# Decoder step with a mixture of experts: last pass's rows added on TensorE, the others' rows added by Pool beside it

## What is computed

```python
def moe_swiglu(h, router, w_gate, w_up, w_down):
    logits = jnp.einsum('btd,de->bte', h, router).astype(jnp.float32)
    top_v, top_i = lax.top_k(logits, TOP_K)
    gate = jax.nn.softmax(top_v, axis=-1)
    combine = jnp.einsum('btk,btke->bte', gate, jax.nn.one_hot(top_i, N_EXPERTS, dtype=jnp.float32))
    out = jnp.zeros(h.shape, jnp.float32)
    for e in range(N_EXPERTS):
        he = jax.nn.silu(h @ w_gate[e]) * (h @ w_up[e])
        out = out + combine[..., e:e + 1] * (he @ w_down[e])
    return out.astype(h.dtype)
```

## Time and profile before

| | us |
|---|---|
| median of 3 runs | 1996.9 (1996.71 to 1997.59) |
| the profiled execution's own time | 1998.28 |
| its span, first to last instruction | 1995.7 |
| TensorE busy in the span | 1961.5 |
| VectorE, ScalarE, POOL busy | 474.0, 298.4, 143.3 |

### The profile page before, as it was taken

How to read it: one execution, slowest core, us unless ns; L and a number is a source line. 1 busy time by engine, 2 the same in 40 slices (tenths; PEclk the granted TensorE clock), 3 DMA queues, 4 the chain that set the end, 5 groups by cost and what they waited for, 6 DMA issues and landing times.

```text
span 1995.7 us, 40349 instructions
## 1 busy us (share of the span) xinstructions
PE 1961.5 (98%) x17109; PEld 1400.9 (70%) x17109; DVE 474.0 (24%) x1223; ACT 298.4 (15%) x741; POOL 143.3 (7%) x246
## 2 busy tenths in 40 slices
PE   8999999999999999999999999999999999999996
PEld 6877777777777777777777476777777675647453
DVE  1353564220000134338433210101001001001011
ACT  2263231100000125422211100000000000000000
POOL 2221011000000000210000300000000000000000
PEclk9999999999999999999999999999999999999998
DMA  9645556464433344554532899999999999999996
GB/s 323 225 164 205 205 175 239 152 233 161 141 133 128 129 146 167 188 193 144 198 130 103 317 415 420 410 419 411 419 413 417 416 413 421 409 421 409 414 420 239
DMA packets 100121, 553.26 MB, mean 277 GB/s; under 512 B 13872, under 2 KB 30288, under 8 KB 41328
## 3 DMA queue, kind: packets, MB, share of 16 engines
q1 hardware_dynamic: 84432, 491.96, 62.9%
q0 software_dynamic: 12720, 48.97, 6.8%
q10 hardware_dynamic: 2800, 9.83, 1.4%
HBM read 532.08 MB, written 24.89 MB: 279 GB/s over the span
## 4 chain that ended last, share of the span: by engine, by line
PE 88%; issue 8%; DVE 2%; DMA 1%; POOL 0%; ACT 0%; POOLq 0%; DVEq 0%; SPq 0%
PE bank L490 38%; PE bank L1052 36%; PE bank L657 3%; PE bank L601 2%; PE bank L688 1%; PE bank L713 1%; PE bank L701 1%; DMA pages<-in_slc_pages 1%; PE bank L541 1%; PE bank L783 1%; PE bank L810 0%; DVE tmp L1916 0%; PE bank L851 0%; PE bank L919 0%; DMA wring<-in_wstream 0%
## 5 line engine op out<-in xcount | busy, mean ns | idle before, releaser
L1052 PE MATMUL bank<-wring,phase_region 128*32 128x512 f32 (+3 forms) x10112 | 868.4, 506 | 0.0
L1052 PEld LDWEIGHTS bank<-wring,phase_region 128*32 128x32 f32 x10112 | 561.7, 110 | 306.5 <-issue 148.2
L490 PE MATMUL bank<-xn,wring 128*128 128x288 f32 x2256 | 567.0, 409 | 9.8 <-DMA wring<-in_wstream 9.2
L490 PEld LDWEIGHTS bank<-xn,wring 128*128 128x128 f32 x2256 | 425.6, 191 | 134.1 <-DMA wring<-in_wstream 9.2
L490 PE MATMUL bank<-phase_region,wring 128*128 128x288 f32 x608 | 148.0, 406 | 0.6 <-DVE phase_region L2096 0.6
L2214 DVE TENSOR_TENSOR tmp<-phase_region,bank 128x512 f32<-128x512 f32 (+1 forms) x48 | 28.6, 595 | 500.9 <-PE bank L1052 500.9
L490 PEld LDWEIGHTS bank<-phase_region,wring 128*128 128x128 f32 x608 | 115.4, 190 | 32.9 <-DVE phase_region L2096 1.1
L1293 ACT ACTIVATE phase_region<-bank 128x512 f32<-128x512 f32 (+14 forms) x124 | 52.8, 464 | 425.2 <-PE bank L1052 296.5
L1584 ACT ACTIVATE phase_region<-bank 128x512 f32<-128x512 f32 (+1 forms) x48 | 26.1, 544 | 531.2 <-PE bank L1052 531.2
L2227 DVE COPY phase_region<-bank 32x256 f32<-32x256 f32 x32 | 13.5, 421 | 263.0 <-PE bank L1052 262.7
L657 PE MATMUL bank<-pages,wring 128*64 128x128 f32 (+1 forms) x1024 | 58.9, 276 | 0.0
(11 more groups left out here) (353 smaller groups left out, 1192.1 us busy)
## 6 DMA issues: line engine op xcount, KB each, us to landing
wring<-in_wstream SPq DMA_DIRECT2D x448, 1024.0 KB, 8.1
y_rows<-phase_region ACTq DMA_DIRECT2D x25, 384.0 KB, 7.5
pages<-in_cmp_pages POOLq DMA_DIRECT2D x64, 128.0 KB, 4.4
pages<-in_cmp_pages SPq DMA_DIRECT2D x64, 128.0 KB, 3.0
pages<-in_slc_pages SPq DMA_DIRECT2D x64, 128.0 KB, 4.4
pages<-in_slc_pages POOLq DMA_DIRECT2D x64, 128.0 KB, 4.8
out_win_keep<-in_win_rows POOLq DMA_DIRECT2D x2, 4064.0 KB, 26.6
pages<-in_win_kT POOLq DMA_DIRECT2D x4, 1024.0 KB, 5.3
```

Source lines behind the costliest of these rows:

```text
L490: mm = nc.tensor.matmul(ps[:, 0:width], wb, rhs(k), start=(k == 0), stop=(k == n - 1))
L1052: mm = nc.tensor.matmul(ps[QT * q:QT * q + QT, out0:out0 + n], lhsT, wring[:, a:a + n], start=start, stop=stop)
```

## The change

The expert whose pass is the last one is treated apart. A token's late row may lie in that pass; for such a token the late row's number is bent to a row of zeros, and its place in the last pass is kept (`rel`). POOL brings these places into a row of 288 numbers on 96 partitions through DRAM (`last_of`, `of_last`), and VectorE compares them with the partition's number (times four, as the constant stands) to a one-hot matrix `one_hot`, 96 x 288. After the loop TensorE multiplies `one_hot` with `yS`, three tiles by two halves of 512 columns, into six banks; the first half waits only for ScalarE's first copy into `yS` (`half_ready`). VectorE adds each product, times `w_late`, to `res`, and SP sends each tile out in two halves.

Both gathers of POOL now wait for the same count of written passes, all but the last, and so follow each other during the last pass, the late one into `pages`. POOL itself multiplies and adds their rows to `res`, twelve operations, and VectorE waits for all of them (`res_sum`) after its loop. At the very end POOL waits for the last pass's rows to be written, which nobody reads any more.

```diff
@@ -302,7 +302,7 @@
         xrow = view(xn_, 0, 3, D // 4)
         xq = view(pages, 0, 3, D)
         res = [view(xn_, D, D), view(oS_, 0, D), view(oC_, 0, D)]
-        early, late = view(reg, 0, 3, D), view(reg, 3 * D, 3, D)
+        early, late = view(reg, 0, 3, D), view(pages, 0, 3, D)
         he = rm(3, NFE * QT)
         xe = rm(3, KD * QT)
         pick = rm(3, CAP)
@@ -320,6 +320,10 @@
         edge = rm(ROW_COLS)
         at_row, at_strip = rm(2 * 3), rm(2 * 3)
         strips = rm(2 * 3, ROW_COLS)
+        of_last = view(reg, rm.at - 2 * 3 * ROW_COLS, T)
+        one_hot = rT
+        base, rel, away = rm(1), rm(3), rm(3)
+        FIN_BANKS = (0, 1, 2, 3, 6, 7)
 
         def C(name, rows=P):
             a, n = CONST_AT[name]
@@ -1098,6 +1102,19 @@
                             mm.then_inc(doneB, 1)
                     assert met[0] == EXP_SLOTS - 1
 
+            pe.wait_ge(S["one_ready"], 1)
+            pe.wait_ge(S["half_ready"], n_it * UNROLL)
+            for hf in range(2):
+                if hf == 1:
+                    for part in range(2):
+                        b, n = loop_released(("dn", part), 0)
+                        per = loop_count(("dn", part), 1) - n
+                        pe.wait_ge(b, n_it * (UNROLL * per) + (n - per))
+                for tt, (t0, n) in enumerate(TILES):
+                    ps = psum[(moe_base[0] + FIN_BANKS[3 * hf + tt]) % 8]
+                    nc.tensor.matmul(ps[0:n, 0:512], one_hot[0:CAP, t0:t0 + n], yS[0:CAP, 512 * hf:512 * hf + 512], start=True, stop=True)\
+                        .then_inc(S["fin"], 1)
+
 
         @block.sync
         def _(sp):
@@ -1164,10 +1181,11 @@
                 pass_slots(i + 1, ex2, 0, RING)
             ex = sp.value_load(passes[0:1, bass.ds(n_pass - 1, 1)], min_val=0, max_val=NE - 1)
             pass_slots(n_pass - 1, ex, RING, EXP_SLOTS)
-            for tt, (t0, n) in enumerate(TILES):
-                sp.wait_ge(S["tile_ready"], tt + 1)
-                sp.dma_start(y_out[t0:t0 + n, :], res[tt][0:n, :]).then_inc(S["y_done"], 16)
-            sp.wait_ge(S["y_done"], 48)
+            for hf in range(2):
+                for tt, (t0, n) in enumerate(TILES):
+                    sp.wait_ge(S["tile_ready"], 3 * hf + tt + 1)
+                    sp.dma_start(y_out[t0:t0 + n, 512 * hf:512 * hf + 512], res[tt][0:n, 512 * hf:512 * hf + 512]).then_inc(S["y_done"], 16)
+            sp.wait_ge(S["y_done"], 6 * 16)
 
 
         @block.gpsimd
@@ -1260,6 +1278,11 @@
             pool.wait_ge(S["scattered"], 6 * 16)
             for q in range(4):
                 pool.dma_start(rows_of[QT * q:QT * q + QT, :], tok_of).then_inc(S["rows_of_in"], 16)
+            pool.wait_ge(S["last_ready"], 1)
+            for tt, (t0, n) in enumerate(TILES):
+                pool.dma_start(last_of[t0:t0 + n, :], rel[0:n, tt:tt + 1]).then_inc(S["last_out"], 16)
+            pool.wait_ge(S["last_out"], 48)
+            pool.dma_start(of_last[0:CAP, :], last_of.rearrange("t o -> o t").to_broadcast([CAP, T])).then_inc(S["last_in"], 16)
             n_it = pool.value_load(passes[0:1, 33:34], min_val=NE // UNROLL, max_val=MAX_PASSES // UNROLL)
             quarter_rows = tok_rows.rearrange("t (q c) -> (t q) c", q=4)
             with pool.Fori(0, n_it) as it:
@@ -1272,11 +1295,23 @@
                             .then_inc(S["xrow_in"], 16)
             for j, (dst, name) in enumerate(((early, "early_in"), (late, "late_in"))):
                 pool.wait_ge(S["turn_ready"], n_it * UNROLL + 1 + j)
-                pool.wait_ge(S["y_rows_out"], n_it * (16 * UNROLL) + 16 * (MAX_PASSES + j))
+                pool.wait_ge(S["y_rows_out"], n_it * (16 * UNROLL) + 16 * MAX_PASSES)
                 nc.gpsimd.tensor_tensor(turn[0:1, 1:2], turn[0:1, 0:1], turn[0:1, 0:1], ALU.add).then_inc(S["turn_ready"], 1)
                 for tt, (t0, n) in enumerate(TILES):
                     pool.indirect_dma_start(dst[0:n, tt, :], None, y_rows, bass.IndirectOffsetOnAxis(ap=row_of[0:n, 3 * j + tt:3 * j + tt + 1], axis=0))\
                         .then_inc(S[f"{name}{tt}"], 16)
+            sums = 0
+            for dst, name, weight in ((early, "early_in", w_early), (late, "late_in", w_late)):
+                for tt, (t0, n) in enumerate(TILES):
+                    pool.wait_ge(S[f"{name}{tt}"], 16)
+                    nc.gpsimd.tensor_tensor(dst[0:n, tt, :], dst[0:n, tt, :], weight[0:n, tt, :].to_broadcast([n, D]), ALU.mult).then_inc(S["res_sum"], 1)
+                    sums += 1
+                    pool.wait_ge(S["res_sum"], sums)
+                    nc.gpsimd.tensor_tensor(res[tt][0:n, :], res[tt][0:n, :], dst[0:n, tt, :], ALU.add).then_inc(S["res_sum"], 1)
+                    sums += 1
+                    pool.wait_ge(S["res_sum"], sums)
+            pool.wait_ge(S["y_rows_out"], n_it * (16 * UNROLL) + 16 * (MAX_PASSES + 1))
+            nc.gpsimd.tensor_tensor(turn[0:1, 1:2], turn[0:1, 0:1], turn[0:1, 0:1], ALU.add).then_inc(S["turn_ready"], 1)
 
 
         @block.scalar
@@ -1585,7 +1620,7 @@
                     act.wait_ge(S["y_rows_out"], i * 16 + BLANKS)
                     act.wait_ge(*loop_filled(("dn", 0), i))
                     ps = psum[loop_bank(("dn", 0))]
-                    copy(yS[0:CAP, 0:512], ps[0:CAP, 0:512])
+                    copy(yS[0:CAP, 0:512], ps[0:CAP, 0:512]).then_inc(S["half_ready"], 1)
                     copy(yS[0:QT, 512:D], ps[CAP:P, 0:512]).then_inc(bank_free[loop_bank(("dn", 0))], 1)
                     act.wait_ge(*loop_released(("dn", 0), i))
                     act.wait_ge(*loop_released(("dn", 1), i))
@@ -2190,7 +2225,6 @@
             link(V.tensor_tensor(w_early, rg2, w_early, ALU.add))
             for j, op in enumerate((ALU.min, ALU.max)):
                 link(V.tensor_tensor(at_row[:, 3 * j:3 * j + 3], rm1.rearrange("p a b -> p (a b)"), rm2.rearrange("p a b -> p (a b)"), op))
-            link(V.tensor_copy(row_of[:, :], at_row))
 
             link(V.tensor_scalar(edge, C("iota")[:, 1:ROW_COLS + 1], float(QT), None, ALU.mult))
             link(V.tensor_tensor(strips, bc(at_row, 2, ROW_COLS), bc(edge, 1, 6), ALU.is_ge))
@@ -2198,10 +2232,21 @@
             link(V.tensor_scalar(at_strip, at_strip, float(QT * ROW_COLS - 1), None, ALU.mult))
             link(V.scalar_tensor_tensor(at_strip, at_row, float(ROW_COLS), at_strip, ALU.mult, ALU.subtract))
             link(V.tensor_copy(scat[:, :], at_strip))
+            link(V.tensor_scalar(base, tabf[:, 32:33], float(CAP), float(-CAP), ALU.mult, ALU.add))
+            link(V.tensor_tensor(rel, at_row[:, 3:6], base.to_broadcast([P, 3]), ALU.subtract))
+            link(V.tensor_scalar(away, rel, 0.0, None, ALU.is_ge))
+            link(V.tensor_scalar(at_strip[:, 3:6], at_row[:, 3:6], -1.0, float(MAX_PASSES * CAP), ALU.mult, ALU.add))
+            link(V.tensor_tensor(away, away, at_strip[:, 3:6], ALU.mult))
+            link(V.tensor_tensor(at_row[:, 3:6], at_row[:, 3:6], away, ALU.add))
+            link(V.tensor_copy(row_of[:, :], at_row))
             signal("rows_ready")
+            link(V.tensor_scalar(rel, rel, 4.0, None, ALU.mult))
+            signal("last_ready")
             n_it = dve.value_load(passes[0:1, 33:34], min_val=NE // UNROLL, max_val=MAX_PASSES // UNROLL)
             dve.wait_ge(S["rows_of_in"], 4 * 16)
             V.tensor_tensor(slot_row[:, :], rows_of[:, 3:6], C("quarter").to_broadcast([P, 3]), ALU.add).then_inc(S["idx_ready"], 1)
+            dve.wait_ge(S["last_in"], 16)
+            V.tensor_scalar(one_hot[0:CAP, :], of_last[0:CAP, :], C("tok_row", CAP)[:, 0:1], None, ALU.is_equal).then_inc(S["one_ready"], 1)
 
             with dve.Fori(0, n_it) as it:
                 for i in [it * UNROLL + n for n in range(UNROLL)]:
@@ -2226,13 +2271,13 @@
                     for q, (t, n0) in enumerate(DN_B):
                         last = V.tensor_copy(yS[QT * t:QT * t + QT, n0:n0 + 256], psum[b][QT * q:QT * q + QT, 0:256])
                     last.then_inc(bank_free[b], 1)
-            for tt, (t0, n) in enumerate(TILES):
-                dve.wait_ge(S[f"early_in{tt}"], 16)
-                link(V.scalar_tensor_tensor(res[tt][0:n, :], early[0:n, tt, :], w_early[0:n, tt, :], res[tt][0:n, :], ALU.mult, ALU.add))
-            for tt, (t0, n) in enumerate(TILES):
-                dve.wait_ge(S[f"late_in{tt}"], 16)
-                V.scalar_tensor_tensor(res[tt][0:n, :], late[0:n, tt, :], w_late[0:n, tt, :], res[tt][0:n, :], ALU.mult, ALU.add)\
-                    .then_inc(S["tile_ready"], 1)
+            dve.wait_ge(S["res_sum"], 12)
+            for hf in range(2):
+                for tt, (t0, n) in enumerate(TILES):
+                    dve.wait_ge(S["fin"], 3 * hf + tt + 1)
+                    ps = psum[(moe_base[0] + FIN_BANKS[3 * hf + tt]) % 8]
+                    r = res[tt][0:n, 512 * hf:512 * hf + 512]
+                    V.scalar_tensor_tensor(r, ps[0:n, 0:512], w_late[0:n, tt, :], r, ALU.mult, ALU.add).then_inc(S["tile_ready"], 1)
 
 
 
```

5 lines of the change are left out of this document (3 added, 2 removed).

## The result

The changed kernel took **2002.06 us** (median of 13 runs, 2000.23 to 2004.12), the kernel before in the same comparison 1998.19 us (13 runs). The ratio is 1.0022, 95% interval 1.0016 to 1.0029: slower by 0.22%, where 1990.9 us and a gain were forecast.

What follows compares the result with a forecast made beforehand. TensorE, 98% busy, and DMA were taken as level in the expert loop, with a tail of waits behind it. 3.3 us lost to the late gather less 9.28 won gives -6.0: 1990.9 us, range 1987.6 to 1995.0.

Steps and rivals of the forecast that it cites:

- Tail, removed and added: After the loop: 13.42 us of row write, wait, gather and sums replaced by 4.14 us, 9.28 us won.
- The closing: From last sum to end of span: output transfer and close of the program, left unchanged at 4.36 us.
- Ahead of the loop: Before the expert loop: POOL's writes and read back take 12.5 us, VectorE ready about 1139; price 0, cover 8 us.
- rival 3: Ahead of the loop: long write and read-back chain makes VectorE late, TensorE lacks free banks, kernel slower; chance 3%.
- The late gather: Last pass: 288 rows, 1.18 MB, gathered behind the early set, delay the weights; 3.3 us lost.
- TensorE's way out of its loop: At loop end: TensorE falls through without a fetch wait; 0 taken, 0.9 us kept for the range.
- POOL's twelve sums: Last pass: two operations per tile and set, 12 us in all, nobody waiting before 1981; price 0.

Runs made afterwards that it cites:

- e1: Changed kernel, but POOL's last wait and small add removed, SyncE waiting for the row write instead: 1995.97 us, 0.9993 of the kernel before.
- e5: Changed kernel with the edits of e1 and e3 together: 1990.1 us, 0.9967 of the kernel before.
- e3: Changed kernel, but the one-hot table made by VectorE alone, without the writes to DRAM and the read back: 1997.59 us, 0.9999 of the kernel before.
- e4: Changed kernel without the three late gathers, POOL's twelve sums kept: 2003.06 us in one run.
- e11: Kernel before plus the unused round trip alone (three four-byte-row writes, read back, and waits): 2002.79 us, 1.0032 of the kernel before.
- e7: Kernel of e5 with the three writes of four-byte rows and POOL's wait put back, no read back: 1995.65 us in one run.
- e8: Kernel of e5 with a read of 288 numbers into each of 96 partitions and VectorE's wait, no tiny writes: 1990.08 us in one run.

## Why the prediction was wrong

Its forecast of -6.0 us held two terms, and both were about right. What failed is two places where a price of 0 was set.

- *Tail, removed and added*: -9.28 forecast, -8.36 measured. The mechanism is right. Six sums took 0.74 to 0.75 us instead of 0.683, and VectorE waited 0.32 and 0.22 us for products, because each product stands as two records of some 0.49 us. The 494 ns of the earlier trace rows was a record, not a product.
- *The closing, "I leave the closing 4.36 us as they are"*: **failed**, +4.97 us. I took those 4.36 us for the output's landing, but in the kernel before SP already waited 2.2 us of them at the end. What bounds the end there is POOL's last instruction plus some 10.3 us, its DRAIN, and the change's last line for POOL, a wait for rows that nobody reads, went into no sum. With POOL free (e1, e5) the closing is 4.3 and 2.1 us.
- *Ahead of the loop, "Price 0; the cover is 8 us"*: **failed**, +3.57 us in the first pass. I asked whether the chain is late for VectorE. It was slower than 12.5 us (19.0 us from POOL's last read of `tok_of`, 1125.81, to VectorE's comparison, which ended at 1144.85), and still VectorE stood idle for 5 us before its first product. What I did not ask is what the chain's transfers do to the other transfers on the same engines, though the earlier trace rows show those as full. The cost was no wait of VectorE but the weights' packets, 119% of the engines' time for 93 of them. So rival 3 had the right place and the wrong mechanism. The same round trip adds 1.35 us to the last pass (114.21 against 112.86).
- *The late gather*: 3.3 forecast, 4.41 measured in the changed kernel, but 112.86 - 109.80 = 3.06 where the ring was not emptied before (e5; 3.08 in e3). The size was right; the rest belongs to the point above.
- *TensorE's way out of its loop*: 0 was right. Its last product of the loop ends at 1983.29, ScalarE's first copy at 1983.48 and its first new product begins at 1983.54; the row names the copy as what ended the 0.25 us between. The rule of the Trainium skill (Runtime: NRT & Kernel Launch, Instruction fetch mechanics), that a taken branch to a target outside the window waits for a fetch, gave 0 for this fall-through, and the trace agrees.
- *POOL's twelve sums*: 0 was right. They took 25.5 us in all (1.9 a multiplication, 2.4 an addition), twice the 12 that were put down for them, and still ended at 1915.11. The last pass took 110.56 us with them (e4) and 110.46 without them (e11), both with the round trip and without a late gather in that pass.

Together: the two terms that were priced make -8.36 + 3.06 = -5.3 us, and e5, the change without the two unpriced costs, has 0.9967 of the time before, -6.6 us (-4.2 to -9.2 by its interval). So the forecast was about one for e5, but that it comes as near as -6.0 is partly luck: e5's closing is 2.2 us shorter than that of the kernel before, a gain that the forecast did not have.

## What to carry to other kernels

Where the DMA engines are full, price a small transfer by what it does to the others, not only by its own time. Here 288 four-byte rows cost the first pass 3.6 to 6.0 us, and the gather of 1.18 MB cost the last one 3.1; yet while 576 such rows went out in a scatter TensorE waited for no weights, so take the price from a run and not from the size. A short chain on VectorE that keeps them in SBUF is the cheaper way. Look at what each engine still has to do at the very end, above all POOL, and give a wait that nobody needs early to an engine that is last anyway. A stall is not over when it ends: a ring of buffers that is nearly level with its user takes hundreds of microseconds to fill up again, and the next burst then costs more.

## What the runs showed of the hardware

- From the end of POOL's last instruction to the end of the span it took 10.3 to 10.6 us in the six kernels with POOL late, whether it was a gather's issue or an add on one element. A record DRAIN of POOL fills that time. In the seven kernels where POOL was done early it is as long, 10.0 to 10.4 us, but is over at least 1.8 us ahead of the end, and there the span ended 2.1 to 4.3 us after the last sum. SP's wait for it stands under another engine's name.
- 288 writes of four bytes from SBUF to DRAM took 9.7 to 12.5 us to land in the changed kernel and e7, and from 1130 to 1135 us the DMA engines stood there at a share of 1.2 with 140 and 189 GB/s, where kernels without the writes (before, e5, e8) moved 384 to 415. The Trainium skill (DMA: Bandwidth & Descriptors, Why small descriptors are slow (HBM only)) gives about three cycles of overhead for each packet and 32 bytes of metadata for each DMA operation. By that 288 would not be seen beside 1 MB loads, and the small packets' own time agrees: 1.1% for all of POOL's queue. What they did to the weights' packets (119% for 93, where 263 took 94%) that overhead does not give; here the measurement decides, and why those packets stood was not found.
- The price of the same writes varied: the first pass took 110.60 to 113.05 us in the six kernels that had them, and 107.02 to 107.17 in the seven profiles without them.
